# Gate and up projections of an fp32 encoder layer: nine of eleven tile pairs as seven quarter products

## What is computed

```
def swiglu(x, w_gate, w_up, w_down):
    return (jax.nn.silu(x @ w_gate) * (x @ w_up)) @ w_down

x = x + 0.5 * swiglu(rmsnorm(x, ffn1_norm[l]), ffn1_w_gate[l], ffn1_w_up[l], ffn1_w_down[l])
h = rmsnorm(x, mix_norm[l]); p = h @ w_in[l]
# differential attention and a Hyena long convolution on parts of p, then
x = x + jnp.concatenate([att_out, hy_out], axis=-1) @ w_out[l]
x = x + 0.5 * swiglu(rmsnorm(x, ffn2_norm[l]), ffn2_w_gate[l], ffn2_w_up[l], ffn2_w_down[l])
return rmsnorm(x, final_norm)
```

## Time and profile before

| | us |
|---|---|
| median of 3 runs | 996.36 |
| span of the profiled execution (first to last instruction) | 995.8 |
| PE busy | 987.3 (99%) |
| PE's weight loads, beside its matmuls | 803.1 |
| DVE busy | 541.1 (54%) |
| ACT busy | 334.5 (34%) |
| first FFN, gate and up tiles | about 5 to 248 |
| its down tiles | about 248 to 368 |
| mixer | about 368 to 624 |
| second FFN | about 624 to 989 |

### The profile page before, as it was taken

The page is one execution under the profiler, slowest core; times in us unless marked ns, Lnnn a source line. Parts: engine busy times, 40 slices in busy tenths (PEclk is TensorE's granted clock), DMA queues, the critical chain, the costliest instruction groups (busy, mean ns, idle before and its releaser), DMA issues.

```text
span 995.8 us, 12064 instructions
## 1 busy us (share of the span) xinstructions
PE 987.3 (99%) x4531; PEld 803.1 (81%) x4531; DVE 541.1 (54%) x776; ACT 334.5 (34%) x498; POOL 28.1 (3%) x36
## 2 busy tenths in 40 slices
PE   9999999999999999999999999999999999999997
PEld 7888888888888887677777878888888888888887
DVE  6645444444554537868888756545444445432332
ACT  6423222232232332244455554322323323222221
POOL 0000000000010101000000000000000000001100
PEclk9999999999999999999999999999999999999999
DMA  6632323222323336121121422222232322233322
GB/s 229 209 105 85 101 90 105 84 105 90 109 85 97 101 116 252 64 85 58 68 83 43 148 96 86 89 101 89 101 105 84 105 92 98 83 112 96 90 63 86
DMA packets 35433, 101.78 MB, mean 102 GB/s; under 512 B 3778, under 2 KB 12111, under 8 KB 35140
## 3 DMA queue, kind: packets, MB, share of 16 engines
q1 hardware_dynamic: 34660, 98.39, 29.3%
q0 software_dynamic: 592, 2.84, 0.8%
q10 hardware_dynamic: 144, 0.05, 0.0%
HBM read 97.04 MB, written 4.22 MB: 102 GB/s over the span
## 4 chain that ended last, share of the span: by engine, by line
PE 94%; DVE 3%; issue 1%; ACT 1%; DMA 0%; DVEq 0%; SPq 0%; ACTq 0%
PE bank L1606 26%; PE bank L1607 26%; PE bank L1608 26%; PE bank L2028 1%; PE bank L2030 1%; PE bank L2029 1%; PE bank L1920 1%; PE bank L1666 1%; PE bank L1667 1%; PE bank L1668 1%; ACT prob L643 0%; PE bank L1747 0%; PE bank L1849 0%; PE bank L1753 0%; PE bank L1749 0%
## 5 line engine op out<-in xcount | busy, mean ns | idle before, releaser
L1606 PE MATMUL bank<-x_hi,w_hi 128*128 128x512 f32 x864 | 340.4, 394 | 0.3
L1608 PE MATMUL bank<-x_hi,w_lo 128*128 128x512 f32 x864 | 336.4, 389 | 0.0
L1607 PE MATMUL bank<-x_lo,w_hi 128*128 128x512 f32 x864 | 336.3, 389 | 0.0
L900 DVE TENSOR_TENSOR w_lo<-raw,w_hi 128x1024 fp32r<-128x1024 f32 (+1 forms) x162 | 196.3, 1211 | 196.9 <-ACT w_hi L477 192.1
L477 ACT CAST w_hi<-raw 128x1024 fp32r<-128x1024 f32 (+1 forms) x162 | 166.2, 1026 | 163.8 <-PE bank L1608 148.7
L1606 PEld LDWEIGHTS bank<-x_hi,w_hi 128*128 128x128 f32 x864 | 162.2, 188 | 39.6 <-issue 6.8
L1608 PEld LDWEIGHTS bank<-x_hi,w_lo 128*128 128x128 f32 x864 | 162.2, 188 | 34.1
L1607 PEld LDWEIGHTS bank<-x_lo,w_hi 128*128 128x128 f32 x864 | 162.3, 188 | 33.1 <-issue 0.7
L1606 PE MATMUL bank<-h_hi,w_hi 128*128 128x512 f32 x330 | 128.4, 389 | 0.0
L1607 PE MATMUL bank<-h_lo,w_hi 128*128 128x512 f32 x330 | 128.4, 389 | 0.0
L1608 PE MATMUL bank<-h_hi,w_lo 128*128 128x512 f32 x330 | 128.4, 389 | 0.0
(11 more groups left out here) (307 smaller groups left out, 777.2 us busy)
## 6 DMA issues: line engine op xcount, KB each, us to landing
raw<-in_ffn_w_gate SPq DMA_DIRECT2D x42, 512.0 KB, 3.2
raw<-in_ffn_w_up SPq DMA_DIRECT2D x42, 512.0 KB, 3.2
raw<-in_ffn_w_down SPq DMA_DIRECT2D x32, 512.0 KB, 3.5
raw<-in_w_in SPq DMA_DIRECT2D x24, 512.0 KB, 3.2
raw<-in_ffn_w_down SPq DMA_DIRECT2D x16, 384.0 KB, 3.1
raw<-in_w_out SPq DMA_DIRECT2D x8, 512.0 KB, 3.4
resid<-in_x_t SPq DMA_DIRECT2D x8, 256.0 KB, 4.9
resid_dram<-resid SPq DMA_DIRECT2D x1, 2048.0 KB, 11.7
```

The costliest lines, as they stand in the source:

```text
L900: nc.vector.tensor_tensor(w_lo[:, half, 0:kb, :], raw[:, slot, 0:kb, :], w_hi[:, half, 0:kb, :].bitcast(F32), ALU.subtract).then_inc(w_spl ...
L1606: nc.tensor.matmul(dst, w_hi[:, half, k, :], hi, start=first and k == 0, stop=False)
L1607: nc.tensor.matmul(dst, w_hi[:, half, k, :], lo, start=False, stop=False)
L1608: ins = nc.tensor.matmul(dst, w_lo[:, half, k, :], hi, start=False, stop=last and k == kb - 1)
```

## The change

Of the 11 pairs of tiles in each FFN, the first two (PLAIN = 4 tiles) stay as they are. Each of the other nine pairs is computed by Strassen's scheme: a pair of gate tiles (256 features) times x (1024 deep, 512 tokens) is cut in quarters (128 features, 512 deep, 256 tokens) and made of seven products instead of eight. The gate tiles of a pair are one *group*, the up tiles another, so an FFN has 18 groups (b = 0 gate, b = 1 up). What changes for each engine:

- PE: a product (`product`) is 4 contraction blocks of 3 matmuls, 256 columns each. Products are called 1, 2, 6, 7, 5, 4, 3, in this order of need; products 1 and 2 of the next group come before product 3 of this one (`seven`, `begin`). Products accumulate in the first half of three PSUM banks per kind of group (`CHAIN_BANKS`), and before the accumulation goes on, the partial result has to be copied or read.
- Right-hand operands (the scaled x and its sums: seven of 128x4x256): made once per FFN. DVE writes x·gain·rinv (`scaled`, 8 instructions of 512), `differences` (2048 elements per partition), `next_difference` and `last_sum` (1024 each); ACT rounds each of the seven (`t_high`, 128x1024), DVE makes the low parts (`t_low`, 128x1024). All of this is queued among the four plain tiles and the first group.
- Left-hand operands (weights and their sums): four sums of 512 elements by DVE per group (`more_sums`), each of the last three waiting for the one before. They are rounded in four parts: a (two quarters, 1024), c (two, 1024), d (two, 1024), e (one, 512), by `high_a`...`high_e` on ACT and `low_a`...`low_e` on DVE, where before there were two parts of 1024 for the same two tiles.
- Outputs: ACT copies three partial results of 128x256 per group (`keep_1`, `keep_2`, `keep_7`), DVE joins them in three instructions of 256 (`upper_near`, `lower_far`, `lower_near`), silu comes in three instructions per pair, the hidden tiles in three (`hidden_a1`, `hidden_b`, `hidden_a2`). No scaling by rinv is left in a group, since x is scaled beforehand.
- The rounding of the 18 hidden tiles made in this way (`high_h` on ACT, `low_h` on DVE, 512 each) moves behind the groups: tiles 4 to 7 beside the last group, 8 to 21 beside the first down tile, with the down tiles' weight splits between them.
- Memory is laid out anew, so the mixer's cosine tables and the one-hot table load after the first FFN's groups (`tables`), semaphores are merged, and the two one-hot products move from among the gate tiles to the second down tile.

The diff, cut to its core:

```diff
--- before.py
+++ after.py
+PLAIN = 4
+I0 = PLAIN // 2
+PAIRS = NF // 2
+GROUPS = 2 * (PAIRS - I0)
+PRODUCTS = 7 * GROUPS
...
+M_OF = {1: 0, 2: 2, 6: 6, 7: 5, 5: 4, 4: 1, 3: 3}
+POS = {6: 0, 7: 1, 5: 2, 4: 3, 1: 4, 2: 5, 3: 6}
+CHAIN_BANKS = ((0, 1, 2), (3, 6, 7))
+EARLY_H = 8
...
+            def sevens(ffn, i, first=False, last=False):
+                high_e(ffn, 0, i)
+                if first:
+                    t_high(ffn, 5)
+                keep_2(ffn, 0, i)
+                if first:
+                    t_high(ffn, 6)
+                high_a(ffn, 1, i)
+                keep_7(ffn, 0, i)
+                gate_a1(ffn, i)
+                high_c(ffn, 1, i)
+                gate_b(ffn, i)
+                high_d(ffn, 1, i)
+                keep_1(ffn, 1, i)
+                high_e(ffn, 1, i)
+                gate_a2(ffn, i)
+                keep_2(ffn, 1, i)
+                if last:
+                    keep_7(ffn, 1, i)
+                    return
+                high_a(ffn, 0, i + 1)
+                keep_7(ffn, 1, i)
+                high_c(ffn, 0, i + 1)
+                high_d(ffn, 0, i + 1)
+                keep_1(ffn, 0, i + 1)
...
+            def strassen(ffn, n_down):
+                high_d(ffn, 0, I0, used_std=n_down)
+                t_high(ffn, 3)
+                t_high(ffn, 4)
+                keep_1(ffn, 0, I0)
+                sevens(ffn, I0, first=True)
+                with act.Fori(I0 + 1, PAIRS - 1) as i:
+                    sevens(ffn, i)
+                sevens(ffn, PAIRS - 1, last=True)
+                high_h(ffn, PLAIN, PLAIN + 2)
+                act.wait_ge(s_used, used(ffn, 1, PAIRS - 1, 1))
+                split(8, n_down)
+                high_h(ffn, PLAIN + 2, EARLY_H)
...
+                    if f == 2:
+                        differences(ffn)
+                    if f == 3:
+                        t_low(ffn, 0)
+                    dve.wait_ge(w_used, n + 1)
                     nc.vector.tensor_tensor(bank[b][:], bank[b][:], rinv[:], ALU.mult).then_inc(gate_scaled, 1)
                     if head:
                         split(8, 4)
+                    if not early and not (first and ffn == 0) and f < PLAIN - 1:
+                        split(8, n + 2)
+                    if f == 1:
+                        scaled(ffn, 4)
+                        scaled(ffn, 5)
+                    if f == 2:
+                        next_difference(ffn)
+                    if f == 3:
+                        t_low(ffn, 1)
+                        low_a(ffn, 0, I0)
+                        more_sums(ffn, 0, I0)
+                        t_low(ffn, 2)
+                    dve.wait_ge(w_used, n + 2)
                     nc.vector.tensor_tensor(bank[2 + b][:], bank[2 + b][:], rinv[:], ALU.mult).then_inc(up_scaled, 1)
                     if early and not head:
+                        split(8, n + 3)
+                    if f == 2:
+                        last_sum(ffn)
+                    dve.wait_ge(gate_act, PLAIN * ffn + f + 1)
+                    dve.wait_ge(up_scaled, PLAIN * ffn + f + 1)
                     nc.vector.tensor_tensor(bank[2 + b][:], bank[2 + b][:], silu[:, b, :], ALU.mult).then_inc(h_made, 1)
+                    if f == 3:
+                        low_c(ffn, 0, I0)
+                    dve.wait_ge(h_hi_made, NF * ffn + f + 1)
+                    nc.vector.tensor_tensor(h_lo[ffn][:, h_place(f), :], bank[2 + b][:], h_high(ffn, f).bitcast(F32),
                                             ALU.subtract).then_inc(h_split, 1)
+                    if f == 0:
+                        for k in range(4):
+                            scaled(ffn, k)
+                    if f == 1:
+                        scaled(ffn, 6)
+                        scaled(ffn, 7)
...
+            def scaled(ffn, k):
+                both = lambda x: x.rearrange("p (t q) -> p t q", t=2)
+                dst = xt_f[ffn][:, 0:2, k, :] if k < 4 else xt_f[ffn][:, 2:4, k - 4, :]
+                nc.vector.scalar_tensor_tensor(dst, both(resid[:, k, :]), col(GAIN[2 * ffn], k), both(rinv[:]),
+                                               ALU.mult, ALU.mult).then_inc(t_made, 1)
+            def differences(ffn):
+                x = xt_f[ffn]
+                dve.wait_ge(t_made, T_OPS * ffn + KD)
+                nc.vector.tensor_tensor(x[:, 4:6], x[:, 0:2], x[:, 1:4:2], ALU.subtract).then_inc(t_made, 1)
...
+            def more_sums(ffn, b, i):
+                dve.wait_ge(b_landed[b], landings(ffn, i, 1))
+                nc.vector.tensor_tensor(sums_23[:, b, 4:8, :], raw[:, 2 * b, 0:4, :], raw[:, 2 * b + 1, 0:4, :], ALU.add).then_inc(more_made, 1)
+                dve.wait_ge(more_made, more(ffn, b, i, 1))
+                nc.vector.tensor_tensor(raw[:, 2 * b + 1, 0:4, :], raw[:, 2 * b + 1, 0:4, :], raw[:, 2 * b + 1, 4:8, :], ALU.add).then_inc(more_made, 1)
+                dve.wait_ge(more_made, more(ffn, b, i, 2))
+                nc.vector.tensor_tensor(sums_23[:, b, 0:4, :], raw[:, 2 * b + 1, 0:4, :], raw[:, 2 * b, 0:4, :], ALU.add).then_inc(more_made, 1)
+                dve.wait_ge(more_made, more(ffn, b, i, 3))
+                nc.vector.tensor_tensor(sums_4[:, b], sums_23[:, b, 0:4, :], raw[:, 2 * b, 4:8, :], ALU.add).then_inc(more_made, 1)
...
+            def sevens(ffn, i, first=False, last=False):
+                if first:
+                    t_low(ffn, 4)
+                low_e(ffn, 0, i)
+                if first:
+                    t_low(ffn, 5)
+                else:
+                    hidden_a2(ffn, i - 1)
+                low_a(ffn, 1, i)
+                if first:
+                    t_low(ffn, 6)
+                more_sums(ffn, 1, i)
+                lower_far(ffn, 0, i)
+                lower_near(ffn, 0, i)
+                low_c(ffn, 1, i)
+                upper_near(ffn, 1, i)
+                low_d(ffn, 1, i)
+                low_e(ffn, 1, i)
+                if not last:
+                    low_a(ffn, 0, i + 1)
+                    more_sums(ffn, 0, i + 1)
+                hidden_a1(ffn, i)
+                lower_far(ffn, 1, i)
+                lower_near(ffn, 1, i)
+                hidden_b(ffn, i)
+                if not last:
+                    low_c(ffn, 0, i + 1)
+                    upper_near(ffn, 0, i + 1)
+                    low_d(ffn, 0, i + 1)
...
+            def strassen(ffn, n_down):
+                t_low(ffn, 3)
+                low_d(ffn, 0, I0)
+                upper_near(ffn, 0, I0)
+                sevens(ffn, I0, first=True)
+                with dve.Fori(I0 + 1, PAIRS - 1) as i:
+                    sevens(ffn, i)
+                sevens(ffn, PAIRS - 1, last=True)
+                low_h(ffn, PLAIN, PLAIN + 2)
+                split(8, n_down)
+                low_h(ffn, PLAIN + 2, EARLY_H)
+                hidden_a2(ffn, PAIRS - 1, last=True)
...
                     for c in range(3):
                         if last and j == 3:
                             continue
+                        if (i, j) == (0, 0):
+                            low_h(ffn, (8, 13, 18)[c], (13, 18, 22)[c])
                         split(CHUNKS[(c + 1) % 3][1], N_STAGE[s] + 3 * j + c + 1, 12, i)
...
+            def product(ffn, which, b, start=False):
+                m = M_OF[which]
+                high, low = operand(POS[which])
+                dst = first_half(CHAIN_BANKS[b][{2: 1, 7: 2, 4: 2}.get(which, 0)])
+                for k in range(4):
+                    nc.tensor.matmul(dst, high[:, k, :], xt_hi[ffn][:, m, k, :], start=start and k == 0, stop=False, skip_group_check=True)
+                    nc.tensor.matmul(dst, high[:, k, :], xt_lo[ffn][:, m, k, :], start=False, stop=False, skip_group_check=True)
+                    ins = nc.tensor.matmul(dst, low[:, k, :], xt_hi[ffn][:, m, k, :], start=False, stop=which in (2, 3, 4) and k == 3,
+                                           skip_group_check=True)
+                ins.then_inc(s_used, 1)
...
+            def begin(ffn, b, i):
+                pe.wait_ge(part_split, fourths(ffn, b, i, "a"))
+                if not (b and isinstance(i, int) and i == I0):
+                    wait(pe, hidden if b else gated, thirds(ffn, i - 1, "a2"))
+                product(ffn, 1, b, start=True)
+                wait(pe, joined, joins(ffn, b - 2, i, "upper"))
+                product(ffn, 2, b, start=True)
...
+            def seven(ffn, b, i, first=False, last=False):
+                if first:
+                    pe.wait_ge(t_split, 7 * ffn + 3)
+                pe.wait_ge(part_split, fourths(ffn, b, i, "c"))
+                pe.wait_ge(kept, held(ffn, b, i, 1))
+                product(ffn, 6, b)
...
+                wait(pe, joined, joins(ffn, b - 2, i, "near"))
+                product(ffn, 7, b, start=True)
+                if first:
+                    pe.wait_ge(t_split, 7 * ffn + 5)
+                pe.wait_ge(part_split, fourths(ffn, b, i, "d"))
+                pe.wait_ge(kept, held(ffn, b, i, 2))
```

(26 more changed lines are left out.)

649 lines of the change are left out of this document (444 added, 205 removed).

## The result

| | before | after |
|---|---|---|
| median of the runs (us) | 996.35 (996.07 to 996.48, 4 runs) | 1006.25 (1005.32 to 1006.56, 4 runs) |
| profiled execution | span 995.8 (its time isn't on record) | 1005.32, span 1003.3 |
| PE busy | 987.3 | 971.3 |
| DVE busy | 541.1 | 714.5 |
| mean granted clock | 1.00 | 0.99 (0.986 to 0.990 in the four runs) |

A forecast was written before the change was run, and what follows sets the result against it. The prediction took PE, busy 987.3 of 995.8 us, as the bound. Its terms, -28.8 + 3.3 + 8.5 + 3.2 + 15.3 + 6.9 + 0.5, gave +8.9: span 1004.7, runs 1005.3 us, range 994 to 1018.

The forecast's parts named there:

- Term 1: PE's work in the groups: 48 full-width matmuls replaced by 84 of 256 columns at 0.120 us, -28.8 us over 36 groups.
- rival (d): Faster: half-width matmuls in long series take 0.109 instead of 0.120 us, giving 991 us; chance 0.13.
- Term 2: Group loop: DVE's chain to the next gate group's `low_c` ties with PE's six products, one 0.2 us restart per pass, +3.3 us.
- Rival (a): DVE paces the group loop, with 0.7 us more per pair over 18 pairs, giving 1018 us; chance 0.20.
- Term 3: Plain tiles: PE waits for weight splits behind DVE's added work, +8.5 us in the first FFN and +3.2 in the second.
- Term 4: Passage from plain tiles into groups: PE waits at product 6, product 3 and the next product 6, +15.3 us in all.
- sign of error: PE's waits at the entries, from plain tiles into groups, together under 15 us would show the prediction wrong.
- Term 5: Passage from groups to down tiles: PE waits 3.9 us in the first FFN, 2.4 in the second; with restarts +6.9 us.
- Term 6: PE's granted clock falling in the three waits longer than 4.9 us: +0.5 us in all, between 0 and 7.
- rival (b): The clock stays down after each long wait, costing 7 us instead of 0.5, about 1012 us; chance 0.08.
- Rival (c): Waits in plain tiles and at groups' entries and exits half as long, 27 instead of 34 us: 998, no change; chance 0.11.

## Why the prediction was right

The time (1005.3 forecast, 1006.25 measured) and the sign were right, and most of it by the steps given. **Term 1**: the half-width step is 0.120 us in series of over a thousand, so rival (d) with 0.109 is out. With it go the estimated 216 and 109 ns that the Trainium skill's formula on the page "TensorE: Matmul & The Clock Gate", section "Back-to-back issue gap", would give here (by it the term would be an estimated -42.8 us; the prediction's -42.6 is a slip).

**Term 2** was right in size and cause. The profile alone could not tell: the idle time stood at the loop's first product and no row of it named DVE. Taking 0.6 us out of the chain cleared it, putting 0.6 us in lengthened each pass by 0.59. Rival (a), DVE as the bound of the loop, is out as long as nothing is added: with DVE busy for 17.0 of 20.37 us, what binds is the one chain.

**Term 3** was 2.7 too large in all. In the first FFN the waits of 1.0 and 6.4 came as 1.0 and 6.2; the 0.9 behind them did not come, because the tile ahead of it ran 1.3 us longer at the lower clock: the split ended at 53.9, and PE came to the tile at about 54.5 instead of 53.2. In the second FFN two of four small waits came.

**Term 4** named the right wait, product 6 for `keep_1` behind ACT's three casts, though the trace named DVE. 5.3 was forecast per FFN, 4.7 and 5.2 came; product 3 waited 0.7 and 0.4 instead of 1.1. The whole was 12.8 instead of 15.3, and PE's waits at the entries together (11.4 by the table of waits) stayed below the 15 that I had set as a sign of error: by that sign the term's sizes were wrong. The chain was right, its small waits too dear.

**Term 5** is right within half a microsecond (its parts with two restarts add up to 6.7 rather than 6.9), with the same causes: moving the split takes 1.1 us off the first FFN's wait and removes the second's 2.4, of which 1.5 come back at the tile's second part.

**Term 6 is the step that failed.** "Most of it falls where PE waits again for DVE" and the +0.5 taken from it were wrong: it was 6.0. I had read the fall after 4.9 us at the kernel's end as if every fall needed that long. It came with waits of 6.2, 4.7, 3.9 and 5.2 us, once (3.9 us, the granted clock 0.68 in the stretch 255 to 256) when PE was already working again, and the low clock held on into 2.7 to 4 us of PE's work each time. One wait alone in the kernel before costs 1.7 to 3.0 us beside itself. That the forecast came within 1 us is luck to this extent: the error was hidden by the 5.9 us that terms 2 to 5 had too much. 6.0 is within the bounds of 0 to 7 given, and rival (b), at 1012, had the size of the clock's cost right. The Trainium skill says on the page "TensorE: Matmul & The Clock Gate", section "What's actually happening", that the throttled clock is the default and activity releases it. That a pause is paid for after it too follows from this, and the trace agrees: 6.0 us in four places.

**Rival (c)**, shorter joints, was nearer in its sizes than I: terms 3 to 5 measured 28.3 us, where I had 34 and it 27 (which is not the half that its heading says). Only the clock's 6.0 kept the time from about 1000. What the changed kernel lost was not in its mathematics: with the joints' work spread and four waits shortened, the same scheme, on one pair less in each FFN, is faster than the kernel before by 1.4%.
